# A group norm whose channel sum is a matmul with a matrix of ones that leaves it in all partitions, and whose power is taken of a whole tile

## The reference

```python
def finish(y, xs, z):
    y = y + xs * d_skip[:, None]
    y = y.reshape(b, n, SSD_DI) * jax.nn.silu(z)
    y = y.reshape(b, n, SSD_GROUPS, SSD_DI // SSD_GROUPS)      # 8 groups of 256 channels
    y = y * lax.rsqrt(jnp.mean(y * y, axis=-1, keepdims=True) + RMS_EPS)
    y = y.reshape(b, n, SSD_DI) * norm_g
    return y @ w_out
```

## Time and profile before

| what | value |
|---|---|
| time, median of 3 runs | 2764.95 us (2759.76 to 2764.98) |
| profiled execution, span | 2760.0 us; no other time of that execution is given |
| PE busy | 2426.7 us, 88% of the span |
| DVE busy | 1471.8 us, 53% |
| ACT busy | 1147.1 us, 42% |
| POOL busy | 605.1 us, 22% |

### The profile page before, as it was taken

One profiled execution on the slowest core, in us unless ns is written; L12 is line 12 of the kernel. 1 busy time (PEld: TensorE's weight loads), 2 busy tenths in 40 slices (PEclk: granted clock), 3 DMA queues, 4 the chain that ended last, 5 costly groups with the idle time before them and its releaser, 6 DMA issues. The chain is left out here.

```text
span 2760.0 us, 36246 instructions
## 1 busy us (share of the span) xinstructions
PE 2426.7 (88%) x12538; PEld 1929.3 (70%) x12538; DVE 1471.8 (53%) x3284; ACT 1147.1 (42%) x2846; POOL 605.1 (22%) x594
## 2 busy tenths in 40 slices
PE   6769989898898989899885999399999999999876
PEld 1338777777777877777664788378878888888555
DVE  1455785859587685858576321613433333333532
ACT  1314545546364645546353111424444444444421
POOL 0011433434243434424241000110110110010000
PEclk8889999999999999999887999599999999999988
DMA  7560001010101001010004431321111211210053
GB/s 259 165 181 31 24 18 52 16 46 16 46 24 39 24 16 54 16 46 16 27 5 160 148 97 54 107 71 31 50 37 53 62 44 33 62 47 16 25 176 98
DMA packets 117261, 172.05 MB, mean 62 GB/s; under 512 B 27576, under 2 KB 78008, under 8 KB 116824
## 3 DMA queue, kind: packets, MB, share of 16 engines
q1 hardware_dynamic: 117080, 169.73, 20.0%
HBM read 141.53 MB, written 30.13 MB: 62 GB/s over the span
## 5 line engine op out<-in xcount | busy, mean ns | idle before, releaser
L599 PE MATMUL sg_pP<-h_h_hi,sg_whi 128*128 128x512 f32 (+1 forms) x1152 | 445.9, 387 | 14.1 <-POOL sg_wlo L1039 14.1
L600 PE MATMUL sg_pP<-h_h_lo,sg_whi 128*128 128x512 f32 (+1 forms) x1152 | 424.7, 369 | 0.0
L601 PE MATMUL sg_pP<-h_h_hi,sg_wlo 128*128 128x512 f32 (+1 forms) x1152 | 424.3, 368 | 0.0
L599 PE MATMUL at_pP<-h_h_hi,at_whi 128*128 128x512 f32 (+1 forms) x640 | 259.0, 405 | 12.0 <-POOL at_wlo L1777 12.0
L599 PEld LDWEIGHTS sg_pP<-h_h_hi,sg_whi 128*128 128x128 f32 x1152 | 232.4, 202 | 47.1 <-POOL sg_wlo L1039 14.2
L600 PEld LDWEIGHTS sg_pP<-h_h_lo,sg_whi 128*128 128x128 f32 x1152 | 231.1, 201 | 32.8
L601 PEld LDWEIGHTS sg_pP<-h_h_hi,sg_wlo 128*128 128x128 f32 x1152 | 229.8, 199 | 34.0
L601 PE MATMUL at_pP<-h_h_hi,at_wlo 128*128 128x512 f32 (+1 forms) x640 | 238.2, 372 | 0.0
L600 PE MATMUL at_pP<-h_h_lo,at_whi 128*128 128x512 f32 (+1 forms) x640 | 237.4, 371 | 0.0
L1777 POOL TENSOR_TENSOR at_wlo<-at_wr,at_whi 128x1024 fp32r<-128x1024 f32 x32 | 75.5, 2358 | 675.0 <-ACT at_whi L1684 675.0
L1737 ACT ACTIVATE at_pm<-at_s,at_nm 128x384 f32<-128x384 f32 x128 | 78.9, 616 | 335.4 <-DVE at_nm L1800 335.4
(11 more groups left out here) (218 smaller groups left out, 5156.2 us busy)
## 6 DMA issues: line engine op xcount, KB each, us to landing
sg_wr<-in_w_ssd SPq DMA_DIRECT2D x48, 512.0 KB, 3.3
at_wr<-in_w_na SPq DMA_DIRECT2D x32, 512.0 KB, 3.8
at_bias<-bt SPq DMA_DIRECT2D x256, 64.0 KB, 2.3
op_yr<-y SPq DMA_DIRECT2D x10, 1024.0 KB, 7.7
md_mod_w<-in_ada_w SPq DMA_DIRECT2D x4, 2048.0 KB, 13.4
nt_mod_w<-in_ada_w SPq DMA_DIRECT2D x4, 2048.0 KB, 10.1
ts_mod_w<-in_ada_w SPq DMA_DIRECT2D x4, 2048.0 KB, 14.2
y<-sg_Z SPq DMA_DIRECT2D x16, 512.0 KB, 3.5
```

What stands on the lines that cost most here:

```text
L599: pe.matmul(out, w_hi[:, k, :], h_hi[:, k, t0:t0 + n], start=(k == 0), stop=False)
L600: pe.matmul(out, w_hi[:, k, :], h_lo[:, k, t0:t0 + n], start=False, stop=False)
L601: x = pe.matmul(out, w_lo[:, k, :], h_hi[:, k, t0:t0 + n], start=False, stop=(k == KT - 1))
```

## The change

The sum over channels becomes a matmul in which the matrix of ones is stationary and sq moves, so the sum of each token is in all partitions at once. var and rstd grow from 128x1 to 128x128, and POOL takes the power of the whole tile. diag and the second matmul go; DVE multiplies Z by rstd from SBUF, in the slot in which the power was taken. One semaphore pair (dg, bcs) goes, and fin takes its place where POOL waits before it overwrites rstd.

```diff
-        var = m.sb("var", [P, 1])
-        rstd = m.sb("rstd", [P, 1])
-        mhalf = m.sb("mhalf", [P, 1])
-        diag = m.sb("diag", [P, P])
+        var = m.sb("var", [P, P])
+        rstd = m.sb("rstd", [P, P])
+        mhalf = m.sb("mhalf", [P, P])
...
                 if g and c == 0:
-                    pe.wait_ge(fin, g * NCH)
+                    pe.wait_ge(vr, g * NCH)
...
             def norms(g, c):
-                if 0 <= c - 2 < NCH:
-                    pe.wait_ge(dg, n - 1)
-                    if n >= 3:
-                        pe.wait_ge(fin, n - 2)
-                    if c == NCH - 1:
-                        pe.wait_ge(ex, n)
-                    pe.matmul(bank[:, P:2 * P], ones[:, :], diag[:, :], start=True, stop=True).then_inc(bcs, 1)
...
                     for t in range(PAIRS):
-                        x = pe.matmul(bank[:, 0:1], sq[:, t * P:(t + 1) * P], ones[:, 0:1], start=(t == 0),
+                        x = pe.matmul(bank[:, 0:P], ones[:, :], sq[:, t * P:(t + 1) * P], start=(t == 0),
                                       stop=(t == PAIRS - 1))
...
                 pool.wait_ge(vr, g * NCH + c + 1)
                 if g or c:
-                    pool.wait_ge(dg, g * NCH + c)
+                    pool.wait_ge(fin, g * NCH + c)
                 pool.tensor_tensor(rstd[:, :], var[:, :], mhalf[:, :], ALU.pow).then_inc(rs, 1)
...
-                    dve.tensor_scalar(var[:, :], norm_bank(c - 1)[:, 0:1], 1.0 / UN, EPS, ALU.mult,
+                    dve.tensor_scalar(var[:, :], norm_bank(c - 1)[:, 0:P], 1.0 / UN, EPS, ALU.mult,
                                       ALU.add).then_inc(vr, 1)
-                if 0 <= c - 3 < NCH:
-                    dve.wait_ge(bcs, n - 2)
-                    for t in range(PAIRS):
-                        zt = Z[:, t, (c - 3) * P:(c - 2) * P]
-                        x = dve.scalar_tensor_tensor(zt, zt, ng[:, g * PAIRS + t:g * PAIRS + t + 1],
-                                                     norm_bank(c - 1)[:, P:2 * P], ALU.mult, ALU.mult)
-                    x.then_inc(fin, 1)
...
             def norm_late(g, c):
                     dve.wait_ge(rs, n - 1)
-                    if n >= 3:
-                        dve.wait_ge(bcs, n - 2)
-                    dve.tensor_scalar(diag[:, :], ident[:, :], rstd[:, 0:1], None, ALU.mult).then_inc(dg, 1)
+                    for t in range(PAIRS):
+                        zt = Z[:, t, (c - 2) * P:(c - 1) * P]
+                        x = dve.scalar_tensor_tensor(zt, zt, ng[:, g * PAIRS + t:g * PAIRS + t + 1],
+                                                     rstd[:, :], ALU.mult, ALU.mult)
+                    x.then_inc(fin, 1)
```

More of the change, by code:

```diff
@@ L693, in ssd_groups @@
         (small, con, whs, wls, pj, pev, t0s, cv, tnh, sil, tA, evA, xdA, stA, scA, auh, aul, arg, ex, mm_,
-         wch, yoff, yoS, yd, xdF, xDs, stF, scF, ysum, fin1, sqs, ssm, vr, rs, dg, bcs, fin, vch, tri, wfw) = map(m.sem, (
+         wch, yoff, yoS, yd, xdF, xDs, stF, scF, ysum, fin1, sqs, ssm, vr, rs, fin, vch, tri, wfw) = map(m.sem, (
              "small", "con", "whs", "wls", "pj", "pev", "t0s", "cv", "tnh", "sil", "tA", "evA", "xdA", "stA",
              "scA", "auh", "aul", "arg", "ex", "mm", "wch", "yoff", "yoS", "yd", "xdF", "xDs", "stF", "scF",
-             "ysum", "fin1", "sqs", "ssm", "vr", "rs", "dg", "bcs", "fin", "vch", "tri", "wfw"))
+             "ysum", "fin1", "sqs", "ssm", "vr", "rs", "fin", "vch", "tri", "wfw"))
         block = ctx.enter_context(nc.Block())
@@ L794, in back @@
                         pe.wait_ge(vr, g * NCH - 2)
-                        pe.wait_ge(fin, g * NCH - 3)
                 if n:
@@ L872, in norms @@
                         pe.wait_ge(vr, n - 1)
+                    if c == NCH - 1:
+                        pe.wait_ge(ex, n)
                     for t in range(PAIRS):
-                        x = pe.matmul(bank[:, 0:1], sq[:, t * P:(t + 1) * P], ones[:, 0:1], start=(t == 0),
+                        x = pe.matmul(bank[:, 0:P], ones[:, :], sq[:, t * P:(t + 1) * P], start=(t == 0),
                                       stop=(t == PAIRS - 1))
@@ L890, in _ @@
                         back_state(g, i)
-                    if g and i < 2:
-                        norms(g - 1, NCH + i)
+                    if g and i == 0:
+                        norms(g - 1, NCH)
                 for c in range(NCH):
@@ L899, in _ @@
             norms(G - 1, NCH)
-            norms(G - 1, NCH + 1)
         @block.scalar
@@ L1272, in _ @@
                     c = s - NCH
-                    if g and s < 3:
+                    if g and s < 2:
                         norm_early(g - 1, NCH + s)
@@ L1296, in _ @@
                         silu(at(step, 2))
-            for c in range(NCH, NCH + 3):
+            for c in range(NCH, NCH + 2):
                 norm_early(G - 1, c)
```

## The result

The changed kernel takes 4375.48 us in the median of 4 runs (4373.99 to 4381.2), the kernel before 2764.12 (2759.76 to 2764.98): a ratio of 1.584 (95% interval 1.582 to 1.586), 58% slower. The profiled execution's span is 4374.7 us, 1614.7 more than before. The direction and the mechanism were as predicted; the likeliest time, 3840, was 535 us too low, inside the range.

A forecast was written before the change was run, and what follows sets the result against it. It took the kernel to be bound by a chain through POOL's 80 powers, in series with the slots. 1016 + 29 - 11 - 23 - 42 + 113 = 1082 us on the 2760.0 span gave 3842, said as 3840; range 2920 to 6200.

The forecast's parts named there:

- Where the power stands: On POOL the power heads a queue: xdb, which PE needs, and xD, which DVE needs, stand behind it.
- The powers are in series: The 80 powers follow one another with a slot's work between; a longer power lengthens the slot as much, less slack.
- The power's duration: POOL's 128-column power takes 13.3 us at 0.1 us per value, 12.7 more than now; 80 times, 1016 us.
- The rival of a power that streams: POOL's power runs at the subtraction's rate, 0.3 us longer: 2761 us, no change; chance 0.07.
- +29: DVE at an unchanged power: larger var and products with Z moved behind L1229, less diag, +0.45 us in 64 forward slots.
- -11: PE's wait of 0.78 us for diag at s = 0 and s = 1 goes, 14 times.
- -23: Slack of xdb at s = 0 and s = 1, seven times 3.24 us, hides part of the power.
- -42: Forward slack, DVE's wait for the slot's last matmul, 41.6 us over 80 chunks, hides part of the power.
- DVE held up by the power: DVE's L1215, with two SBUF inputs, would be held until the power ends, at no further cost.
- The clock: PE's clock drops after each wait: 1.7 us in 40 forward slots, 2.8 in 16 backward ones, +113 us.
- Overlaps well: POOL's power costs 0.02 to 0.05 us per value: 2977 to 3335 us; chance 0.25 for 2920 to 3335.
- does not overlap: POOL's power costs 0.3 to 0.41 us per value: 5870 to 6990 us; chance 0.30 for more than 0.2.

The follow-up runs named there:

- experiment 2: Kernel before with var, rstd and the power 128 columns wide, only the first used, its old norm otherwise kept: 4377.42 us, ratio 1.585.
- experiment 1: Changed kernel with the power taken of only 1, 16 or 64 of 128 columns: 2761.66, 2930.66 and 3552.66 us.
- experiment 3: Changed kernel with 80 added 512-column matmuls on PE before the wait for xdb in forward slots c = 2 to 8: 4334.29 us, ratio 1.570.

## Why the prediction was right, point by point

- *Where the power stands.* Right. It was read from the order of POOL's queue and from one slot; the waits of after name xdb and xD with up to 21 us each, and experiment 2 gives the whole loss with nothing but the width.
- *The powers are in series.* Right: a group grew by 201 us for ten powers that are 202 us longer in all. The prediction's sign was ten times the excess less about 6 us; it was less about 1.
- *The power's duration.* This is the term that was mis-sized. 0.1 us per column was taken, between 0.0024 and 0.41; measured are 0.159. The tile takes 20.8 us, not 13.3. At 80 powers this is 600 us; the sum was too low by 533, the rest being terms that were too high (below, the small terms). A value above the geometric middle was the right side, but the reason given for it (an engine overlaps only a few steps of a power) is not shown. A single column takes 0.57 us, and the line through the widths splits it into 0.41 once and 0.16 per column; columns taken strictly one after the other, with that cost once, give the same line. Between bounds that lie a factor of 170 apart, that the forecast came within a factor of 1.6 is in part luck.
- *The two rules of the Trainium skill.* The Trainium skill, GPSIMD Engine Reference, section 3.1, gives 2.6 cycles per element for a two-input instruction. That fits the subtraction roughly (2483 ns for 1024 columns) and not the power, which costs 66 times as much per column. Section 7 of that page of the Trainium skill, with its factor of about 4 between one dependent chain and interleaved ones, gives an estimate of 0.1 from the 0.41, near the 0.159. No run here shows that this is why: the 0.41 is mostly what a power costs once.
- *The restructured norm itself.* The rival of a power that streams came out, by its other terms, at 2761, no change; experiment 1 with one column has 2761.66. The main sum's own terms for that case, +29 and -11, would make it 18 us slower; the interval of experiment 1 is -2 to +3 us. The terms of +29, -11, -23 and -42 us were not measured one by one.
- *DVE held up by the power.* Wrong, without a cost. L1207, with two SBUF inputs, was to be held until the power ends; it ran in 0.42 us in its first microsecond.
- *The clock.* Right that it drops in each place, too high in price where it was measured: the prediction has 68 us for the forward slots, and 38 to 41 came back in experiment 3, whose matmuls stand in 56 of the 64 and removed the drop in most of them.
- *The small terms together.* Behind the power the prediction adds +29, -11, -23, -42 and +113 us, +66 in all (without the clock 47 us hidden; its paragraph on the streaming rival says 46). Measured is a sum of -3 to -7, so these terms were too high by about 70. With the 38 to 41 us of the clock that experiment 3 gave back, 41 to 48 us of a longer power would be hidden without that drop, which fits the 47. What the drop costs in the backward slots no run shows, so this fit is not proof.
- *The rivals.* "Overlaps well" (0.02 to 0.05 us per value, to 3335 us) and "does not overlap" (0.3 to 0.41, from 5870 us) are both out by the measured 0.159, in their prices. Whether columns overlap at all stays open, as said above.

## What to carry to other kernels

Before a small operation is widened, ask for its price per element on that engine, and whether the trace has it at more than one width: one row at width 1 can't tell 0.002 us per element from 0.4, and here the range was as wide as that. Then read the engine's own queue behind it, not its busy share: POOL was idle 95 of 157 us per group and still had no room ahead of xdb and xD. If a factor is needed in all partitions, take the expensive function of the narrow form and spread its result; the gain lay in which engine does the cheap step between (ACT instead of DVE, 1.1%).

## What the runs showed of the hardware that was not expected

- A power on POOL costs 0.159 to 0.160 us per column of 128 partitions, from 16 to 128 columns, and about 0.4 us once (a single column took 568 ns in the mean).
- It did not hold up DVE here: a DVE product of 256 columns with both inputs in SBUF that started 0.55 us into a power took 0.42 us (1201.75), and none of that line's 80 took over 0.69; beside POOL's subtraction a product of 128 columns took 2.46. So what a POOL instruction does to DVE depends on which one it is.
- The length of the last wait does not decide PE's clock. After waits of 1.95 to 1.96 us in the same place of the slot order it fell to half in four groups of the kernel before and stayed full in one; after the same waits with diag on ACT it stayed full in 17 of 18.
